# Hybrid decoder trunk on one core: the first weight chunk taken tile by tile, and VectorE's selection rounds of block 1 regrouped

## The reference

```python
h = rms_norm(x, pre_w, NORM_EPS)
proj = jnp.einsum('bsd,dn->bsn', h, w_in)           # n = 9*512 + 64 + 8
dq, dk, dv, dg, sq, sk, sv, sg, iq, ik, iw = jnp.split(proj, SPLIT_OFFSETS, axis=-1)
# group A: differential attention, 4 heads, two 64-wide maps per head (rope on dq, dk)
oa = diff_attention(dq, dk, dv, lam)                # softmax0 - lam * softmax1, causal
oa = rms_norm(oa, subln_w, SUBLN_EPS) * (1.0 - lambda_init) * silu(dg)
# group B: sparse attention, 4 heads of 128 (rope on sq, sk, iq, layer-normed ik)
score = einsum('bqhk,bqh->bqk', relu(einsum('bqhd,bkd->bqhk', iq, ik)), iw)   # causal
_, idx = lax.top_k(score, 64)                       # 64 keys chosen for each query
ob = softmax(sq . k[idx] * scale, masked) . v[idx] * silu(sg)
y = jnp.einsum('bsm,md->bsd', concat([oa, ob]), w_out)
return x + rms_norm(y, post_w, NORM_EPS)
```

## Time and profile before

| | us |
|---|---|
| median of 3 runs | 309.3 |
| the profiled execution | 309.01 |
| its span, first to last instruction | 307.1 |
| PE busy | 295.2 (96%) |
| DVE busy | 238.0 (77%) |
| ACT busy | 165.0 (54%) |
| POOL busy | 73.5 (24%) |

### The profile page before, as it was taken

One profiled execution on the slowest core, in us unless ns is written; L12 is line 12 of the kernel. 1 busy time (PEld: TensorE's weight loads), 2 busy tenths in 40 slices (PEclk: granted clock), 3 DMA queues, 4 the chain that ended last, 5 costly groups with the idle time before them and its releaser, 6 DMA issues.

```text
span 307.1 us, 4427 instructions
## 1 busy us (share of the span) xinstructions
PE 295.2 (96%) x1588; PEld 248.6 (81%) x1588; DVE 238.0 (77%) x482; ACT 165.0 (54%) x290; POOL 73.5 (24%) x116
## 2 busy tenths in 40 slices
PE   8899999999999899999999999999999989999992
PEld 7699777788787688888888988778878768888892
DVE  4853999799999977883984786878999999688233
ACT  5986854644776274502675855473657727560101
POOL 5648800302032311001060730021303040110001
PEclk9999999999999999999999999999999999999998
DMA  7999959457518488121049799926652856200011
GB/s 242 372 370 387 357 201 383 134 103 268 196 23 254 137 266 283 45 54 59 1 154 365 251 335 282 320 81 176 215 183 82 209 186 191 102 2 0 0 70 68
DMA packets 48951, 56.87 MB, mean 185 GB/s; under 512 B 21921, under 2 KB 26529, under 8 KB 48929
## 3 DMA queue, kind: packets, MB, share of 16 engines
q1 hardware_dynamic: 48640, 56.06, 56.3%
q10 hardware_dynamic: 288, 0.52, 0.5%
HBM read 52.91 MB, written 3.67 MB: 184 GB/s over the span
## 4 chain that ended last, share of the span: by engine, by line
PE 66%; DVE 24%; ACT 3%; DMA 2%; POOL 2%; issue 2%; SPq 0%; POOLq 0%; DVEq 0%; ACTq 0%
PE bank_a L435 12%; PE bank_a L426 11%; PE bank_a L431 11%; DVE w_lo L948 8%; PE bank_a L572 7%; PE bank_s L572 6%; DVE work L1063 4%; PE bank_o L549 3%; DVE top L1062 3%; PE bank_t L405 3%; PE bank_a L443 3%; DVE xt_pbuf L1080 2%; DVE xt_pbuf L1096 2%; DMA w_raw<-in_w_in 2%; ACT xt_pbuf L790 2%; PE bank_s L532 2%
## 5 line engine op out<-in xcount | busy, mean ns | idle before, releaser
L948 DVE TENSOR_TENSOR w_lo<-w_raw,w_hi 128x2048 fp32r<-128x2048 f32 (+1 forms) x46 | 99.1, 2165 | 18.8 <-ACT w_hi L718 18.6
L718 ACT ACTIVATE w_hi<-w_raw 128x2048 fp32r<-128x2048 f32 (+1 forms) x46 | 81.9, 1785 | 34.7 <-PE bank_a L435 26.5
L435 PE MATMUL bank_a<-w_lo,h_hi 128*128 128x512 f32 (+1 forms) x272 | 70.3, 380 | 2.5 <-DVE w_lo L948 2.5
L426 PE MATMUL bank_a<-w_hi,h_hi 128*128 128x512 f32 (+1 forms) x272 | 72.7, 389 | 0.0
L431 PE MATMUL bank_a<-w_hi,h_lo 128*128 128x512 f32 (+1 forms) x272 | 70.0, 379 | 0.0
L435 PEld LDWEIGHTS bank_a<-w_lo,h_hi 128*128 128x128 f32 x272 | 49.5, 188 | 13.3 <-DVE w_lo L948 3.8
L431 PEld LDWEIGHTS bank_a<-w_hi,h_lo 128*128 128x128 f32 x272 | 49.8, 188 | 9.8
L426 PEld LDWEIGHTS bank_a<-w_hi,h_hi 128*128 128x128 f32 x272 | 47.8, 188 | 10.3 <-issue 2.7
L1388 POOL TENSOR_TENSOR rt<-nat,tab 128x256 f32<-128x256 f32 x10 | 7.4, 741 | 112.4 <-ACT nat L774 112.3
L790 ACT ACTIVATE xt_pbuf<-xt_pbuf,st 128x128 f32<-128x128 f32 (+1 forms) x48 | 21.3, 444 | 19.1 <-DVE st L1080 19.1
L774 ACT ACTIVATE nat<-bank_a,st 128x512 f32<-128x512 f32 x20 | 13.5, 681 | 19.6 <-PE bank_a L435 19.6
(11 more groups left out here) (198 smaller groups left out, 450.3 us busy)
## 6 DMA issues: line engine op xcount, KB each, us to landing
w_raw<-in_w_in SPq DMA_DIRECT2D x30, 1024.0 KB, 5.8
w_raw<-in_w_out SPq DMA_DIRECT2D x8, 1024.0 KB, 5.0
w_raw<-in_w_in SPq DMA_DIRECT2D x8, 584.0 KB, 7.0
turned<-mixn SPq DMA_DIRECT2D x20, 128.0 KB, 2.7
w_raw<-in_w_in SPq DMA_DIRECT2D x3, 512.0 KB, 6.8
prm<-in_rows SPq DMA_DIRECT2D x2, 705.0 KB, 6.2
xres<-in_x SPq DMA_DIRECT2D x2, 512.0 KB, 9.7
dqT<-turned SPq DMA_DIRECT2D x2, 512.0 KB, 5.9
```

The costliest lines, as they stand in the source:

```text
L426: pe.matmul(bank, h_hi[:, HALF * half + kk, tok], whi[:, kk, :], start=half == 0 and kk == 0, stop=False)
L435: mm = pe.matmul(bank, h_hi[:, HALF * half + kk, tok], wlo[:, kk, :], start=False, stop=half == 1 and kk == HALF - 1)
L718: act.activation(unit(w_hi, u), unit(raw, u), ACT.Copy).then_inc(hi_done.sem, 1)
L948: dve.tensor_tensor(unit(w_lo, u), unit(raw, u), unit(w_hi, u).bitcast(F32), ALU.subtract).then_inc(lo_done.sem, 1)
```

## The change

Two parts.

*The opening.* k tile 0 of chunk 0 is fetched as two halves of 256 columns ("corners") from ACT's queue; k tiles 1, 2 and 3 are fetched one by one from SP's queue, between the pieces of the transposed x. The second half of the chunk stays two pieces of two k tiles. The transposed x is laid out k tile by k tile with both blocks side by side, so h_hi and h_lo are made by one 128x256 instruction for each k tile instead of two of 128x128. PE takes the three products for both blocks, tile by tile (for tile 0: corner by corner, 256 columns at a time). One warm-up matmul fewer.

*The regrouping*, in both layers. The eight rounds of block 1 become packs of 1, 2, 2, 2 and 1 instead of 3, 2 and 3; split_lo(17) moves ahead of the last three rounds, the drain of T_PD1A and combine(10) ahead of the last round and the mask.

```diff
-WARM_UP = 8
+WARM_UP = 7
@@ SyncE
             turned(0)
             turned(1)
+            first_tile(1, tile_landed[1])
             turned(2)
-            sp.dma_start(piece(raw, 0, 1), weights(0, 0)[:, FIRST_TILES:HALF, :]).then_inc(raw_landed[0].sem, 16)
+            first_tile(2, tile_landed[2])
+            first_tile(3, raw_landed[0].sem)
             turned(3)
@@ TensorE
+                    for c in range(2):
+                        part = slice(c * SPLIT, (c + 1) * SPLIT)
+                        pe.wait_ge(corner_hi[c], 1)
...
+                    for k in range(1, SINGLE):
+                        pe.wait_ge(turned_hi, k + 1)
+                        if k < SINGLE - 1:
+                            pe.wait_ge(tile_hi, k)
+                        else:
+                            pe.wait_ge(hi_done.sem, 1)
+                        for b in range(BLOCKS):
+                            step(h_hi, w_hi, b, [k])
...
@@ ScalarE
-            act.dma_start(tile(raw, 0), weights(0, 0)[:, 0:1, :]).then_inc(tile_landed[0], 16)
+            for c in range(2):
+                act.dma_start(corner(raw, c), w_in[0, 0:P, c * SPLIT:(c + 1) * SPLIT]).then_inc(corner_landed[c], 16)
             act.wait_ge(neg_half_ready, 1)
             act.activation(spare, neg_half[:, 0:1], ACT.Sin)
-            act.dma_start(tile(raw, 1), weights(0, 0)[:, 1:2, :]).then_inc(tile_landed[1], 16)
             act.wait_ge(xt_landed[0], 16)
-            turned(0, 0)
+            turned(0)
+            high(lambda ring: corner(ring, 1), corner_landed[1], corner_hi[1])
...
@@ VectorE, both layers
-                choose(1, 3)
+                choose(1, 1)
                 drain_pair(T_DK, dkT)
+                choose(1, 2)
                 split_lo(layer, 15)
...
                 mask_scores(11, 1, 2, causal[:, :])
-                choose(1, 3)
+                split_lo(layer, 17)
+                choose(1, 2)
+                drain(T_PD1A, pT[:, 1, :])
+                combine(10, 1, 2, 2)
+                choose(1, 1)
                 mask_unchosen(1)
-                drain(T_PD1A, pT[:, 1, :])
-                split_lo(layer, 17)
-                combine(10, 1, 2, 2)
                 drain_pair(T_SK, skT)
```

More of the change, by code:

```diff
@@ L439, in opening, with step @@
                 def opening():
-                    def step(x, w, b, ks, stop=False):
+                    def step(x, w, b, ks, stop=False, part=slice(0, WIDTH)):
                         for k in ks:
-                            mm = pe.matmul(A[b][:, :], x[:, k, b * P:(b + 1) * P], w[:, k // HALF, k % HALF, :],
-                                           start=x is h_hi and w is w_hi and k == 0, stop=stop and k == KT - 1)
-                        return mm
-                    for k in range(FIRST_TILES):
-                        pe.wait_ge(turned_hi, k + 1)
-                        pe.wait_ge(tile_hi[k], 1)
-                        step(h_hi, w_hi, 0, [k])
-                        pe.wait_ge(turned_lo, k + 1)
[L452 to L463, removed]
+                            mm = pe.matmul(A[b][:, part], x[:, k, b * P:(b + 1) * P], w[:, k // HALF, k % HALF, part],
+                                           start=x is h_hi and w is w_hi and k == 0 and part.start == 0, stop=stop and k == KT - 1)
@@ new lines, in step @@
+                        return mm
+                    for c in range(2):
+                        part = slice(c * SPLIT, (c + 1) * SPLIT)
+                        pe.wait_ge(corner_hi[c], 1)
+                        pe.wait_ge(turned_hi, 1)
+                        for b in range(BLOCKS):
+                            step(h_hi, w_hi, b, [0], part=part)
+                        pe.wait_ge(turned_lo, 1)
+                        for b in range(BLOCKS):
+                            step(h_lo, w_hi, b, [0], part=part)
+                        pe.wait_ge(corner_lo, c + 1)
+                        for b in range(BLOCKS):
+                            step(h_hi, w_lo, b, [0], part=part)
@@ L464, in opening @@
+                    mm.then_inc(first_half_used.sem, 1)
+                    for q in range(2, KT // FIRST_TILES):
+                        ks = range(FIRST_TILES * q, FIRST_TILES * (q + 1))
+                        pe.wait_ge(turned_hi, FIRST_TILES * (q + 1))
                         if q == 2:
@@ L466, in opening @@
                         else:
[L467 to L472, removed]
+                            pe.wait_ge(hi_done.sem, 2)
+                        for b in range(BLOCKS):
+                            step(h_hi, w_hi, b, ks)
+                        pe.wait_ge(turned_lo, FIRST_TILES * (q + 1))
+                        for b in range(BLOCKS):
+                            step(h_lo, w_hi, b, ks)
                         if q == 2:
@@ L475, in opening @@
                         else:
[L476 to L484, removed]
+                            pe.wait_ge(lo_done.sem, 2)
+                        for b in range(BLOCKS):
+                            mm = step(h_hi, w_lo, b, ks, stop=True)
+                            if q == 3:
+                                mm.then_inc(proj_done.sem, 1)
                 def first(g):
@@ L735, in square_x, with turned, high @@
                                accum_out=ms_x[:, b:b + 1]).then_inc(x_squared.sem, 1)
[L737 to L746, removed]
+            def turned(k):
+                act.activation(h_hi[:, k, :], xt[:, x_at(k):x_at(k + 1)], ACT.Copy, scale=pre[:, 0, k:k + 1]).then_inc(turned_hi, 1)
+            def high(part, landed, done):
+                act.wait_ge(landed, 16)
+                act.activation(part(w_hi), part(raw), ACT.Copy).then_inc(done, 1)
             def body(layer):
@@ new lines, in low @@
+            def low(part, hi, n, done):
+                dve.wait_ge(hi, n)
+                dve.tensor_tensor(part(w_lo), part(raw), part(w_hi).bitcast(F32), ALU.subtract).then_inc(done, 1)
+            dve.wait_ge(corner_landed[0], 16)
+            dve.tensor_copy(corner(w_hi, 0), corner(raw, 0)).then_inc(corner_hi[0], 1)
+            low_turned(0)
+            low(lambda ring: corner(ring, 0), corner_hi[0], 1, corner_lo)
+            low(lambda ring: corner(ring, 1), corner_hi[1], 1, corner_lo)
```

110 lines of the change are left out of this document (51 added, 59 removed).

## The result

| | before | after |
|---|---|---|
| median of 4 runs, us | 309.27 (309.02 to 309.4) | 303.81 (303.61 to 304.2) |
| ratio, 95% interval | | 0.9826 (0.9809 to 0.9843) |
| span of the profiled execution, us | 307.1 | 301.8 |

The account below looks back on a forecast made before the run. PE, busy 96% of the span, was taken as the bound, with time to gain only from its waits. 309.01 - 3.3 (both layers) - 0.15 (opening) = 305.55, forecast as a 305.7 us median, range 304.0 to 307.7.

Parts of the forecast that it names:

- The two waits, 2.44 us a layer: PE's waits for the dkT drain (0.90 us) and the w_lo of unit 17 (1.54 us) go in each layer.
- Both ties: PE just meets POOL's rope at the T_SK transposes (100.28 against 100.4) and DVE's drains at scores of 12 (104.33 against 104.3).
- The new wait of 0.75 us at gate_dsa(0): At turn_mix(T_MS0), PE at 129.26 finds DVE's gate ending at 130.0: about 0.75 us lost a layer.
- only about 0.6 us earlier: gate_diff(0) and gate_diff(1) follow DVE's own scores through ACT's exponentials, so they gain about 0.6 us.
- rival 1: The new wait at gate_dsa(0) does not come, POOL and ACT answering faster: 5.0 us less, 304.2; chance 0.15.
- the size 0.15: Of 1.05 us gained in the opening by 17 us, 0.15 us comes through the splits at unit 7.
- The stop of about 1 us that I named at unit 7: PE's w_lo pack of unit 7 starts between 34.5 and 35.0 after a new wait of about 1 us.
- the case that the rope has passed: At unit 7, POOL's rope is over before DVE's split, which ends at 34.4: 0.5 us of the opening comes through.
- Rival 5, the clock in the opening: Shorter warm-up and waits between tiles keep TensorE at 1.2 GHz; 315.6 if the whole opening runs slow; chance 0.04.

Follow-up runs that it names:

- the late split: Kernel after with two selection rounds ahead of the split of unit 17 instead of behind it: 307.44 us.
- the early combine: Kernel after with the last three rounds grouped 1 and 2 around combine(10) instead of 2 and 1: 304.64 us.
- the two memsets: Kernel after with two memsets of 128x512 put on VectorE ahead of gate_dsa(0): 306.18 us.
- the regrouping alone: Kernel before with VectorE's rounds regrouped at both places in both layers and the old opening: 304.37 us.
- the first place: Kernel before with only the dkT drain moved behind one round, the other two rounds behind it: 310.78 us.
- the second place: Kernel before with only the split of unit 17 moved ahead of the last three rounds, the dkT drain as before: 305.92 us.
- the opening alone: Kernel after with both places of VectorE's rounds put back as before, keeping the changed opening: 308.67 us.

## Why the prediction was wrong

**The two waits, 2.44 us a layer: right.** 2.38 were measured, and both went.

**Both ties: right.** PE's transposes of T_SK started at 99.81 behind a rope that ended at 99.64, and its scores of 12 at 103.86, with no wait at either. That the rope would take 0.74 us was the step they rested on, and the late split shows its price: 3.6 us of median (307.44 - 303.81, across two comparisons), of which the rope has 2 x 1.5. The ties were won by little: 0.17 us at the rope and, with the drains of T_SK over at 103.52, 0.34 at the scores of 12; the early combine used up the second. The Trainium skill (SBUF — State Buffer, Who interferes with whom) has a VectorE instruction with two SBUF inputs and a GpSimd one that reads SBUF take turns; the traces agree, in both directions: POOL's instruction 1.9 us longer beside a split, DVE's 0.5 us longer beside the rope.

**The new wait of 0.75 us at gate_dsa(0): wrong, and this is the step that failed.** I wrote that the gates of block 0 and 1 come "only about 0.6 us earlier", and that gate_dsa(0) ends at 130.0. Each place in layer 0, with the 0.53 us of the opening taken off the measured move:

| | before | after | forecast | measured less 0.53 |
|---|---|---|---|---|
| split of unit 18 | 104.61 | 103.43 | -0.4 | -0.65 |
| gate_diff(0) | 114.67 | 112.76 | -0.6 | -1.38 |
| gate_diff(1) | 123.21 | 121.30 | -0.6 | -1.38 |
| gate_dsa(0) | 130.14 | 127.39 | -1.3 | -2.22 |
| PE, turn_mix(T_MS0) | 131.70 | 128.79 | -1.7 | -2.38 |

The rows of before for the first two, from its timeline, with ACT's move and POOL's first product ahead of the gate:

```profile
104.61 2.28 DVE L948 TENSOR_TENSOR w_lo<-w_raw,w_hi 128x2048 fp32r<-128x2048 f32 x1
...
111.53 0.69 ACT L774 ACTIVATE v_diff<-bank_a,st 128x512 f32<-128x512 f32 x1 [1.04 <-PE bank_a L435]
...
113.33 0.20 POOL L1374 TENSOR_TENSOR st<-st 128x4 f32<-128x4 f32 x1 [11.11 <-ACT mixn L798]
...
114.67 1.13 DVE L1106 SCALAR_TENSOR_TENSOR mixn<-bank_o,st,gate 128x128 f32<-128x128 f32 x4 [1.47 <-POOL st L1375]
```

The missing 0.78 us at gate_diff have three sources.

- 0.25 at the split of unit 18. From the split of unit 17 on I summed DVE's drawn durations to 8.85 us; the rows after give 103.43 - 94.83 = 8.60. The split, drawn 2.29, is followed by the next instruction after 2.20; the drain of 0.69 by the combine after 0.61. I had made this correction for PE (0.16 us a pack) and not for DVE. 0.05 of the 0.25 is a slip of mine: 99.65 + 0.65 is 100.30, and I went on from 100.35.
- 0.26 between that split and DVE's own scores of 12. I counted 0.2 us of short waits for PE as gone; DVE needed 3.26 us for that stretch before and 2.80 after, 0.46 less: the 0.20 in the bracket leaves out what the drawn ends hide.
- 0.27 on the way through ACT and POOL. I held the squares of ACT to DVE's pace alone. ACT had also waited for PE there (1.04 us before a move out of bank_a), and PE was 2.4 us earlier: the squares start at 109.32 instead of 112.12, 2.27 us earlier without the opening. Most of that did not reach the gate. POOL's first product behind the squares now meets DVE's split of unit 20 (the second of the two in the row, over at 111.56), takes 1.11 us instead of 0.20 and ends at 111.62:

```profile
107.07 4.49 DVE L965 TENSOR_TENSOR w_lo<-w_raw,w_hi 128x2048 fp32r<-128x2048 f32 x2
...
110.51 1.11 POOL L1377 TENSOR_TENSOR st<-st 128x4 f32<-128x4 f32 x1 [10.88 <-ACT mixn L817]
```

So in the kernel after DVE's split sets gate_diff(0) by way of POOL, at 255.69 us of layer 1 as well. Without the meeting the gate could come up to 0.9 us earlier still (1.11 - 0.20, an estimate from these rows); no run tests that.

The last 0.14 to the 0.92 at gate_dsa(0) lie behind gate_diff(1), where the wait for w_hi went as I had said. That DVE's pace passes whole to the gates is shown by the early combine (+0.57 at all of them), and that gate_dsa(0) is where it reaches PE by the two memsets. A wait of 0.75 us was the difference of two moves, 2.44 and 1.3, each with an error of its own; the second was wrong by 0.92, and the sign turned. Over two layers it is 2 x (2.38 - 1.65) = 1.5 us, most of the 1.9 us between forecast and result. It was rival 1 that came about, at 304.2 us, with a chance of 0.15. The reason that I gave for it, a faster answer of POOL and ACT, has 0.27 of the 0.92; 0.51 lie on DVE's own list. It deserved about as much as the forecast: my reason against it was just the 0.6.

**The opening: right that most of it is lost at the splits, the size 0.15 where 0.53 came.** Chunk 0 ended at 16.74 instead of 16.5; the 24 matmuls took 5.68 us where I had 5.5 (my own 8.43 us for 36 gives 5.62). The gap ahead of them is 0.1 us and not 0.6, since the corners ran at the lower level and ended later. The stop of about 1 us that I named at unit 7 did not come, and the pack started at 34.43, ahead of my 34.5 to 35.0: PE lost 0.31 us at the w_lo of unit 6 and 0.28 at unit 7, restarts counted, where the kernel before lost 0.31 at unit 7 alone, and 0.82 - 0.31 - 0.28 + 0.31 is the 0.53 within rounding. I had 34.4 for the case that the rope has passed, and that is what the trace of the kernel after shows. How DVE's splits and POOL's rope meet also differs between kernels with one and the same opening. PE's first work behind unit 7 starts at 36.00, 35.75, 36.17 and 35.92 us with the old opening (before, the regrouping alone, the first place, the second place) and at 35.47, 35.76, 35.30, 35.54 and 35.50 with the new one (after, the opening alone, the late split, the two memsets, the early combine). The means are 0.45 us apart, with 0.4 us of spread in either group, so the 0.53 and the 0.24 of single traces are one effect as far as these runs can tell; the medians of the opening alone say 0.3 (308.99 to 308.67).

**Rival 5, the clock in the opening:** it showed in small, 2.3 us at 1.2 GHz, and cost nothing that lasts, since it lies ahead of the wait for k tiles 4 and 5 (with 8 warm-up matmuls the second half starts no earlier). It would have decided only from 4.5 us on.

**The range** ended at 304.0 and left out part of rival 1, whose own time of 304.2 lay at its edge. With the opening's upper bound (0.5) and no wait at the gate the forecast's own terms give 309.01 - 4.88 - 0.5 = 303.6; that is the low end that followed from them.

## What to carry to other kernels

When an edit moves two engines by different amounts, the new wait at the next place where they meet is a difference of two estimates: work out every term of the slower engine from start to start, as carefully as for the one that gains, and where the difference is under the errors, give "no wait" the same weight. Look for the waits that an engine in the middle (here ACT) had for the engine that is now earlier; they shrink too, and what they give back may be taken by a new meeting (here POOL's product and DVE's split). And place instructions that share a path with another engine (here DVE's long splits and combine, POOL's rope) by when the other runs: the same instructions in another order differed by 3.6 us.

## What the runs showed of the hardware

- The clock fell behind one wait of 2.07 us and not behind another of the same length in the same execution; behind six waits of 1.24 to 1.33 us in three other kernels (before, the opening alone, the late split) it did not. Where it fell it cost 1.6 us, nearly as much as the wait.
- In the opening the matmuls ran at 1.2 GHz up to 6.47 us in a stretch whose granted clock is given as 1.00; the spacing of the matmuls told it, the column did not.
- POOL's rope beside DVE's selection rounds cost neither anything: the rounds took 0.42 and 0.41 us, the rope's instructions 0.75, 0.47, 0.46. Beside the split the rope's instruction took 2.7 us, beside the rope the combine's instruction on 128x2 elements 0.71 instead of 0.22, and beside a split POOL's product of 128x4 elements 1.11 instead of 0.20.
